# Latent attention on one Trainium2 core: rotary query columns made once and kept in DRAM, plain query columns shared by two heads

## The reference

```python
c_q   = proj[..., :768]                      # latent queries
c_kv  = proj[..., 768:1024]                  # latent keys and values
k_rope = proj[..., 1024:1056]
q  = (_rms(c_q, mla_q_norm[j]) @ mla_w_q_up[j]).reshape(b, s, 12, 96)
kv = (_rms(c_kv, mla_kv_norm[j]) @ mla_w_kv_up[j]).reshape(b, s, 12, 64 + 64)
k  = concatenate([kv[..., :64], k_rope of every head], -1)
v  = kv[..., 64:]
q, k = _rms(q, mla_g_qn[j]), _rms(k, mla_g_kn[j])          # over all 96 columns of a head
q = concatenate([q[..., :64], _rope(q[..., 64:], positions)], -1)
k = concatenate([k[..., :64], _rope(k[..., 64:], positions)], -1)
o = causal softmax attention(q, k, v)        # 12 heads
```

## Time and profile before

| | us |
|---|---|
| median of three runs | 2635.06 |
| lowest and highest of them | 2631.56, 2637.10 |
| the profiled execution, its own time | 2625.39 |
| its span in the trace | 2623.7 |
| mean granted TensorE clock in it | 0.986 |

### The profile page before, as it was taken

One profiled execution on the slowest core, in us unless ns is written; L12 is line 12 of the kernel. 1 busy time (PEld: TensorE's weight loads), 2 busy tenths in 40 slices (PEclk: granted clock), 3 DMA queues, 4 the chain that ended last, 5 costly groups with the idle time before them and its releaser, 6 DMA issues. The chain is left out here.

```text
span 2623.7 us, 37082 instructions
## 1 busy us (share of the span) xinstructions
PE 2510.2 (96%) x12000; PEld 2041.3 (78%) x12000; DVE 1739.9 (66%) x2659; ACT 1312.3 (50%) x2483; POOL 1112.8 (42%) x839
## 2 busy tenths in 40 slices
PE   7989999989999999999988999999799999999999
PEld 5767777667788888888777777778687888888887
DVE  6667787855766666478654377777648665665495
ACT  6566777745433333444654366666545333333443
POOL 2034554311466566555311432332003665565554
PEclk9999999999999999999999999999899999999999
DMA  4111110153223232664302000000242323234843
GB/s 145 45 29 33 33 33 9 33 177 112 81 102 106 96 116 84 238 235 149 103 23 57 14 20 22 21 21 21 88 161 91 117 100 104 100 112 141 287 126 117
DMA packets 182795, 242.74 MB, mean 93 GB/s; under 512 B 31376, under 2 KB 105872, under 8 KB 182672
## 3 DMA queue, kind: packets, MB, share of 16 engines
q1 hardware_dynamic: 182672, 241.19, 27.6%
HBM read 175.60 MB, written 65.54 MB: 92 GB/s over the span
## 5 line engine op out<-in xcount | busy, mean ns | idle before, releaser
L2374 POOL TENSOR_TENSOR l0s_run_lo<-l0s_run,l0s_run_hi 128x512 fp32r<-128x512 f32 (+2 forms) x120 | 143.4, 1195 | 216.0 <-DVE l0s_run_hi L2527 216.0
L471 POOL TENSOR_TENSOR l1f_wd_lo<-l1f_d,l1f_wd_hi 128x512 fp32r<-128x512 f32 x77 | 107.9, 1402 | 105.6 <-ACT l1f_wd_hi L546 105.6
L471 POOL TENSOR_TENSOR l0f_wd_lo<-l0f_d,l0f_wd_hi 128x512 fp32r<-128x512 f32 x77 | 110.1, 1431 | 96.5 <-ACT l0f_wd_hi L546 96.4
L84 PE MATMUL banks<-l0f_T_hi,l0f_op_hi 128*128 128x512 f32 x352 | 137.2, 390 | 1.3 <-DVE l0f_T_lo L691 1.3
L84 PE MATMUL banks<-l1f_T_hi,l1f_op_hi 128*128 128x512 f32 x352 | 137.2, 390 | 1.3 <-DVE l1f_T_lo L691 1.3
L86 PE MATMUL banks<-l1f_T_hi,l1f_op_lo 128*128 128x512 f32 x352 | 137.0, 389 | 0.0
L86 PE MATMUL banks<-l0f_T_hi,l0f_op_lo 128*128 128x512 f32 x352 | 137.0, 389 | 0.0
L85 PE MATMUL banks<-l1f_T_lo,l1f_op_hi 128*128 128x512 f32 x352 | 136.9, 389 | 0.0
L85 PE MATMUL banks<-l0f_T_lo,l0f_op_hi 128*128 128x512 f32 x352 | 136.9, 389 | 0.0
L433 POOL TENSOR_TENSOR l1f_s<-l1f_raw 128x512 f32<-128x512 f32 x44 | 66.7, 1516 | 155.9 <-DMA l1f_raw<-in_w_ffn_gu_dram 134.3
L503 ACT ACTIVATE l1f_op_hi<-l1f_s 128x512 fp32r<-128x512 f32 x88 | 55.2, 632 | 140.4 <-PE banks L86 140.4
(11 more groups left out here) (534 smaller groups left out, 8371.6 us busy)
## 6 DMA issues: line engine op xcount, KB each, us to landing
l0f_raw<-in_w_ffn_gu_dram SPq DMA_DIRECT2D x22, 1024.0 KB, 5.0
l1f_raw<-in_w_ffn_gu_dram SPq DMA_DIRECT2D x22, 1024.0 KB, 5.0
l0f_a_raw<-hidden_rows SPq DMA_DIRECT2D x77, 256.0 KB, 3.9
l1f_a_raw<-hidden_rows SPq DMA_DIRECT2D x77, 256.0 KB, 3.6
hidden_rows<-l0f_hid SPq DMA_DIRECT2D x44, 256.0 KB, 2.0
l0f_d<-in_w_ffn_down_dram SPq DMA_DIRECT2D x44, 256.0 KB, 5.1
hidden_rows<-l1f_hid SPq DMA_DIRECT2D x44, 256.0 KB, 2.0
l1f_d<-in_w_ffn_down_dram SPq DMA_DIRECT2D x44, 256.0 KB, 4.9
```

The source lines that it names most:

```text
L84: pe.matmul(out, l_hi, r_hi, start=first, stop=False, skip_group_check=True)
L471: pool.tensor_tensor(wd_lo[g % RING][:], held[HELD_AT[DOWN[p][1]]][i][:], as_f32(wd_hi[g % RING][:]), ALU.subtract).then_inc(wd_lo_done, 1)
L2374: pool.tensor_tensor(run_lo[x % NR][:, f:HALF], run[x % NR][:, f:HALF], as_f32(run_hi[x % NR][:, f:HALF]), ALU.subtract).then_inc(run_spli ...
```

## The change

1. The plain columns of both heads of a pair lie side by side in one 128-column unit. A pair has two query units (one for each half of the sequence) in place of four, in two parts of nine matmuls: 36 matmuls in place of 72.
2. The rotary columns of all 12 heads are made once, in the opening: six units "rope b half" (four heads of 32 columns fill 128) of 18 matmuls. ScalarE squares each, VectorE multiplies it with two tables (plain and swapped order) into `rope_out` and `swap_out`, and SyncE stores both in DRAM (`rotary_query_rows`). "rss b half" sums the squares with four matmuls 128x4; VectorE adds the constant and keeps the sums (`base_all`), which go to DRAM (`query_norm_base`).
3. For each pair SyncE loads the rotary rows back into rows 64 to 127 of `q32` (three loads for each head) and the pair's part of the sums (`base`, one load). The plain columns get their gain on the way out of PSUM: head 0 on VectorE, head 1 on ScalarE. "qhi u" on ScalarE then makes the high part of a unit.
4. "ss half" is four matmuls of 128x2 with the squares as the stationary side. The result stands in the right layout, and the transposes and ScalarE's copy go. "rq half" on VectorE adds `base`.
5. The weights of a pair are split by one instruction on each engine.
6. `extras`, `OPENING` and `POOL_ORDER` are new. In the loop the query units stand in steps 0 to 4 alone; "ksum 1" and "knorm 1" move from step 7 to steps 10 and 11; the key transposes stand in steps 11, 13, 14 and 16 (10, 11, 18 and 21 before).

The diff, cut to its core:

```diff
+    mem = Memory(nc, at, OPENING_AT)
+    q32 = Memory(nc, at - S * 4, 229344)(f"{tag}_q32", [P, 2, S])
+    q_sq = [mem(f"{tag}_q_sq{s}", [P, HALF]) for s in range(2)]
...
-    PARTS = ((0, 2), (2, 4), (4, 6))
...
-    extras = {0: ["q 0 0", "q 0 1"], 1: ["v1", "q 0 2"], 3: ["kv 0"], 4: ["kv 1"], 5: ["kv 2", "ksum 0"],
-              6: ["kv 3", "knorm 0", "wk"], 7: ["q 1 0", "ksum 1", "q 1 1", "q 1 2", "knorm 1"], 8: ["ss 0"],
-              9: ["rq 0"], 10: ["kturn 0"], 11: ["kturn 1"], 12: ["qnorm 0", "q 2 0", "wq 0"], 13: ["q 2 1", "v0"], 15: ["q 2 2"],
-              16: ["q 3 0"], 17: ["q 3 1", "q 3 2"], 18: ["wq 1", "kturn 2"], 19: ["ss 1"],
-              20: ["rq 1", "qnorm 1"], 21: ["kturn 3"]}
...
+    PARTS = ((0, 3), (3, 6))
+    ROPES = [(b, half) for b in range(3) for half in range(2)]
...
+    OPENING = ["kv 0", "kv 1", "kv 2", "kv 3", "wr 1", "rope 0 0", "ksum 0", "rope 0 1", "knorm 0", "rss 0 0", "q 0 0", "ksum 1",
+               "rss 0 1", "q 0 1", "knorm 1", "ss 0", "kturn 0", "q 1 0", "rq 0", "q 1 1", "qhi 0", "qnorm 0", "kturn 1", "ss 1",
+               "wr 2", "rope 1 0", "S", "qhi 1", "rq 1", "S", "qnorm 1", "S", "rope 1 1", "S", "rss 1 0", "kturn 2", "S", "qhi 2",
+               "rss 1 1", "S", "kturn 3", "S", "qhi 3", "S", "S", "rope 2 0", "wq", "wk", "rope 2 1", "rss 2 0", "v0", "rss 2 1"]
+    extras = {0: ["q 0 0"], 1: ["v1", "q 0 1"], 2: ["ss 0", "rq 0"], 3: ["q 1 0"], 4: ["q 1 1"], 5: ["ss 1", "rq 1", "qhi 0"],
+              6: ["kv 0", "wq"], 7: ["kv 1", "qhi 1"], 8: ["kv 2", "ksum 0"], 9: ["kv 3", "knorm 0"], 10: ["ksum 1", "qnorm 0", "wk"],
+              11: ["knorm 1", "kturn 0"], 13: ["kturn 1", "v0"], 14: ["qhi 2", "kturn 2"], 15: ["qnorm 1"], 16: ["qhi 3", "kturn 3"]}
...
@@ SyncE
+            def load_rotary(h, g):
+                for first, kind, row, n in ((HD, 0, 0, ROPE), (HD + ROPE, 1, H, H), (HD + ROPE + H, 1, 0, H)):
+                    sp.dma_start(q32[first:first + n, h, :], rope_dram[kind, bass.ds(g * 2 * ROPE + h * ROPE + row, n), :]).then_inc(rope_in[h], 16)
...
+            def turn(g, last=False):
+                if not last:
+                    load(g + 2)
+                sp.wait_ge(q_read, 2 * g + 2)
+                load_base(g + 1)
+                for h in range(2):
+                    sp.wait_ge(q_split, 4 * g + 2 * h + 2)
+                    load_rotary(h, g + 1)
+                for n in range(4):
+                    at_.store_job(sp, n, g)
...
@@ VectorE
+                elif kind == "rope":
+                    dve.tensor_tensor(rope_out[0][r % 2][:], bank_of(what, g)[:], tables[0][:, cols], ALU.mult)
+                    dve.tensor_tensor(rope_out[1][r % 2][:], bank_of(what, g)[:], tables[1][:, cols], ALU.mult).then_inc(rope_copied, 1)
...
                 elif kind == "rq":
...
+                    half = int(n[0])
+                    dve.wait_ge(ss_made, 2 * g + half + 1)
+                    src = bank_of(f"ss {half}", g)[:, 0:2 * HT].rearrange("p (i a) -> p a i", a=2)
...
+                        dve.wait_ge(base_in, 16 * g)
+                        add = base[:, half, :, :]
+                    dve.tensor_tensor(q_dev[:, group(half)].rearrange("p (a i) -> p a i", a=2), src, add, ALU.add).then_inc(q_read, 1)
...
@@ TensorE, unit "ss"
-                    for half in range(2):
-                        last = pe.matmul(bank_of(what, g)[half * HD:(half + 1) * HD, :], ones[:], q_sq[half][:],
+                    for i in range(HT):
+                        last = pe.matmul(bank_of(what, g)[:, 2 * i:2 * i + 2], q_sq[half][:, i * P:(i + 1) * P], twos[:],
                                          start=True, stop=True, skip_group_check=True)
```

More of the change, by code:

```diff
@@ L1244, in begin, with store_job @@
             sp.sem_inc(s, 16)
+    def store_job(self, sp, n, turn=0):
+        h, half = self.jobs[n]
+        sp.wait_ge(self.out_done, 1 + turn * self.nj + n + 1)
+        sp.dma_start(self.store(h, half, turn), self.o_out[n % 2][:]).then_inc(self.stored[n % 2], 16)
     def sync(self, sp, turn=0):
-        for n, (h, half) in enumerate(self.jobs):
-            sp.wait_ge(self.out_done, 1 + turn * self.nj + n + 1)
-            sp.dma_start(self.store(h, half, turn), self.o_out[n % 2][:]).then_inc(self.stored[n % 2], 16)
+        for n in range(self.nj):
+            self.store_job(sp, n, turn)
     def stores(self, turns):
@@ new lines, in load_base, with store_rotary, spread_table @@
+            def load_base(g):
+                sp.dma_start(base[:].rearrange("p a h i -> p (a h i)"), base_dram[:, bass.ds(g * G, G)]).then_inc(base_in, 16)
+            def store_rotary(r):
+                b, half = ROPES[r]
+                sp.wait_ge(rope_copied, r + 1)
+                for kind in range(2):
+                    sp.dma_start(rope_dram[kind, b * P:(b + 1) * P, columns(half)], rope_out[kind][r % 2][:]).then_inc(rope_stored[r % 2], 16)
+            def spread_table():
+                for n in range(4):
+                    for kind, row, first, count in ((0, HD, 0, ROPE), (1, HD + ROPE + H, 0, H), (1, HD + ROPE, H, H)):
+                        at_row = n * ROPE + first
+                        sp.dma_start(tables[kind][at_row:at_row + count, :], table[row:row + count, :]).then_inc(spread, 16)
@@ L3096, in step @@
                     lower_values(1, 2 * g - 1)
-            lower_queries(0, 0)
-            lower_queries(1, 0)
-            for what in POOL_ORDER:
-                if what != "v1":
-                    step(what, 0)
+            lower_rotary_weights(0)
+            lower_queries(0)
+            for what in POOL_FIRST:
+                step(what, 0)
             with pool.Fori(1, PAIRS - 1) as g:
@@ L3106, in _ @@
             for what in POOL_ORDER:
-                if what not in ("wq 0", "wq 1", "wk"):
+                if what not in ("wq", "wk"):
                     step(what, PAIRS - 1)
@@ L3313, in prepare @@
                     last.then_inc(kv_made, 1)
+                elif kind == "rope":
+                    b, half = int(n[0]), int(n[1])
+                    if half == 0:
+                        pe.wait_ge(wr_lo, b + 1)
+                    free(what, g)
+                    for c in range(NQ):
+                        last = product3(pe, bank_of(what, g)[:], wr["hi"][b % 2][:, c, :], wr["lo"][b % 2][:, c, :],
+                                        cq["hi"][:, c, columns(half)], cq["lo"][:, c, columns(half)], c == 0, c == NQ - 1)
+                    last.then_inc(rope_made, 1)
+                elif kind == "rss":
+                    r = 2 * int(n[0]) + int(n[1])
+                    if r == 0:
+                        pe.wait_ge(made_ones, 2)
+                    free(what, g)
+                    pe.wait_ge(rope_squared, r + 1)
+                    for i in range(HT):
+                        last = pe.matmul(bank_of(what, g)[:, 4 * i:4 * i + 4], q_sq[r % 2][:, i * P:(i + 1) * P], fours[:],
+                                         start=True, stop=True, skip_group_check=True)
+                    last.then_inc(rss_made, 1)
@@ L3314, in prepare @@
                 elif kind == "q":
-                    u, part = int(n[0]), int(n[1])
-                    h, half = halves[u]
-                    unit = f"q {u} 0"
+                    half, part = int(n[0]), int(n[1])
+                    unit = f"q {half} 0"
                     if part == 0:
                         if half == 0:
-                            pe.wait_ge(wq_lo[h], g + 1)
+                            pe.wait_ge(wq_lo, g + 1)
+                            if isinstance(g, int) and g == 1:
+                                for s in range(2):
+                                    pe.wait_ge(rope_stored[s], 96)
```

302 lines of the change are left out of this document (186 added, 116 removed), and 3 rows, old and new, of the table OPENING.

## The result

The changed kernel takes 2704.57 us (median of 4 runs, 2702.8 to 2710.9), the kernel before 2634.44: **1.0275 times as long, 95% interval 1.0262 to 1.0289**, 70 us more where 13 were forecast. The profiled execution's span grew from 2623.7 to 2701.1 us, by 77.4.

The account below looks back on a forecast made before the run. TensorE was taken to bound steps 0 to 9, VectorE steps 10 to 23 after the change. Stretch B -22, base wait +12, stretch A +1, opening +22 made +13 on 2625.4; with 9.7 for the median, 2648 us, range 2622 to 2668.

Parts of the forecast that it names:

- Stretch B: Steps 10 to 23 of a loop turn, 36.2 us before: forecast 31.8 us, -4.4 us a turn (-5.8 to -3.3).
- 28.9 / 0.92 = 31.4 us: Between the split halves of steps 10 and 22: VectorE's 28.9 us of work, filled to 92% as in the closing turn.
- the margins: Time before the half of step 10 and behind that of step 22: 3.1 us before, half kept, 1.5 us.
- The base wait: Step 2 of four turns: VectorE, then TensorE, waits for the late-loaded norm table, 3.0 us each, +12 us (0 to +15).
- The low end of the sum: The forecast's own lower bound: 2635.1 - 29 + 10 + 1 + 18 = 2635 us.
- The clock: Rival, chance 0.22: the base stall drops TensorE's clock to 0.52 for 7.0 us, 3.4 us a turn, +13, 2661 us.
- a clock that falls in both stretches: Case beyond the range: TensorE's clock falls in steps 0 to 9 and 10 to 23; chance some 0.06.
- Stretch A: Steps 0 to 9 of a loop turn, 27.6 us before: keeps 36 query matmuls, gets both new sums, +0.25 us a turn.
- The opening: Before the loop, 41.0 us: rotary matmuls and sums added, query matmuls removed, +20.2 us plus 2 us, +22 (18 to 26).
- the way through DRAM: In the opening, first scores wait for a store (2.3 us) and a load (3.6 us), partly covered: 2 us added.
- The faster rival: VectorE's work slides into steps 0 to 9: 9.3 us a turn gained, 2606 us, or 2622 for half; chance 0.14.

Follow-up runs that it names:

- e5: e4 with another plan of score tiles, tiles 12 to 15 of a pair made by the end of steps 5 to 9 instead of 9 to 13: 2695.56 us.
- e3: Kernel before the change with 30 query matmuls a turn (6.8 us, steps 12 to 17) left out, nothing else changed: 2637.91 us for 2630.45.
- e1: Changed kernel with the load of the norm's base issued some 50 us ahead of its use, behind the first output store of an earlier turn: 2686.04 us.
- e2: e1 with 36 more 128x512 matmuls a turn on TensorE that serve nothing, ahead of the transposes of steps 13 to 18: 2686.64 us.
- e4: e1 with the preparation spread over the turn: second query unit at steps 12 and 13, keys, values, second key norm and key transposes at old steps: 2668.37 us.
- e9: e4 with rotary units and sums between the opening's score tiles, and the first product of a head's half behind the step's scores: 2653.58 us.

## Why the prediction was wrong

*Stretch B: -4.4 us a turn forecast, +3.7 measured (+18.5 in five).* This is the step that failed: "28.9 / 0.92 = 31.4 us", with 1.5 us of margin around it. The work itself was met. Between the same two split halves, those of steps 10 and 22 (1737.34 and 1771.96), VectorE is busy for 29.0 us:

```profile
1737.30:1772.00 34.70, 26.03 (x133) 22.72 (x134) 29.03 (x72) 19.33 (x42) 8.38 (x8) 0.80 0.03 8
```

But these take 34.7 us and not 31.4: VectorE is filled to 84% and not to the 92% of the closing turn. And the margins are 5.0 us, where the prediction halved 3.0 to 1.5. Those two, 3.2 and 3.5 us, and the 1.1 us by which 31.8 was set under 32.9 make up the distance from 31.8 to the 39.6 us of this turn. In the margin stands a product that was not counted: keys and values went from steps 3 to 6 to 6 to 9, so the first key norm's product fell into stretch B too, and its four instructions (1.2 us) stand ahead of the half of step 10.

VectorE's work was not the bound at all. e5 took work from VectorE without gain; e3 took only matmuls, and VectorE was at 83%. What holds the stretch is the way of a block through TensorE, ScalarE and VectorE in order, with one bank at the end of a half. The query matmuls of steps 12 to 17 were the cover of its waits at steps 14 and 18: a sum of durations of 8.2 us in the forecast, nothing as time in e3 (6.8 us of them). The third wait, at step 12, was made by the move of keys, norms and weights, whose effect on ScalarE's queue the prediction put at nothing.

*The base wait: +3.0 us in four turns forecast; 2.1 to 3.1 measured.* Right in place, releaser and size; the load was issued at 1708.68 and used 3.6 us later, the upper bound of the earlier trace rows. The low end of the sum is not the text's: the text allows for no stall at all, the sum takes +10 us; with nothing it would be 2625 in place of 2635.

*The clock* was the rival with 0.22. It came at its place: after the stall a query matmul took 0.43 us. e1 prices stall and clock at 5.3 us a turn, against 3.0 + 3.4 in the text, which took 7.0 us at the lower level where 4.1 were measured. But it was no rival of the forecast: both happened, and its price was to be added. Behind the waits of stretch B the clock fell also (0.83), the case of "a clock that falls in both stretches" that got some 0.06. Its price there is not settled: e2's filler gained 0.7 us net, e4's two kinds of turn say some 2 us. The Trainium skill ("TensorE: Matmul & The Clock Gate", What's actually happening) lets the clock follow TensorE's recent activity; the trace agrees for both stretches, with the falls behind waits of 3.04, 2.94 and 3.55 us in the turn shown.

*Stretch A otherwise: +0.25 forecast, +1.1 measured* (e1: 28.7 us); TensorE waits 0.95 us for VectorE's copy of the query unit ahead of the new sum.

*The opening: +22 (18 to 26) forecast, +29.6 measured.* The 20.2 us for the matmuls were near: e9's opening is 20.0 us longer than that of before, with 21.4 us more of TensorE's work and 1.4 us less of idle time. Undersized was what lies between: four waits of 1.3 to 2.1 us for exponentials, since the rotary units of the last third stood behind the score tiles and covered none. The prediction added 2 us for the way through DRAM and nothing for these. In turn 0 the stores of the rotary rows added a wait of 1.7 us and the low clock behind it, in stretch A.

*The faster rival* (a slide of VectorE's work into stretch A) did not happen: VectorE is busy for 14.6 us in stretch A of after, for 19.9 before; with the new list stretch A holds less of its work, not more. (TensorE's 51.4 us for such a turn should read 51.1, 60.5 less 9.35; nothing hangs on it.) The range ended at 2668, so it missed the time by 37 us.

## What to carry to other kernels

Before matmuls are counted as gained, ask what stood behind them: where a wait by another engine's chain ends in the same steps, they are its cover, and a run with them left out (e3) prices the edit before it is built. Stalls that left TensorE idle for 2.1 to 3.1 us cost their own length and some 2 to 3 us of low clock on top (e1), so such a price is added to the forecast, not held as a rival. When units move, count what each engine's queue holds on both sides of the stretch, ScalarE's in-order copies too.

## What the runs showed of the hardware

TensorE's clock fell to the lower level right behind idle times of 2.1 to 3.1 us in stretch A (granted clock 0.50 from 1712.4 to 1716.5), and matmuls of 512 columns then started 0.43 us apart for 0.227. Behind the 2.94 us wait at step 12 it fell 1.3 us later, at about 1744.1. An idle time of that length is not needed: in e2 it fell in stretch A of two turns with no wait longer than 1.0 us in it, and did not in two others with the same waits. Work of TensorE that nobody needs (e2) raised the granted clock of stretch B from 0.83 to 0.96, and the stretch took 38.8 us for 39.5. The load of 8 KB in rows of 64 bytes took as long from issue to use (3.6 us) as one of 256 KB to landing.
